# Rotary scores of the first attention in rounded high and low parts, with the query's high part copied across the partitions

## The reference, cut to what matters

```
q_nope, q_rope = q[..., :128], q[..., 128:]                       # per head, 128 and 64
q_rope, k_rope = axial_rope(q_rope, angles), axial_rope(k_rope, angles)
q = concatenate([q_nope, q_rope]);  k = concatenate([k_nope, broadcast(k_rope)])
s = einsum('bqhd,bkhd->bhqk', q, k) * (128 + 64) ** -0.5          # float32
p = softmax(s);  o = einsum('bhqk,bkhd->bqhd', p, v)
```

## Time and profile before

| | |
|---|---|
| median of three runs | 2628.06 us |
| profiled execution, its own time | 2628.91 us |
| its span (first to last instruction) | 2627.1 us |
| PE busy | 2589.2 us, 99% |
| DVE busy | 1780.0 us, 68% |
| ACT busy | 1212.4 us, 46% |
| mean data rate | 208 GB/s |
| mean granted clock of PE | 0.997 |

### The profile page before, as it was taken

One profiled execution on the slowest core, in us unless ns is written; L12 is line 12 of the kernel. 1 busy time (PEld: TensorE's weight loads), 2 busy tenths in 40 slices (PEclk: granted clock), 3 DMA queues, 4 the chain that ended last, 5 costly groups with the idle time before them and its releaser, 6 DMA issues.

```text
span 2627.1 us, 37181 instructions
## 1 busy us (share of the span) xinstructions
PE 2589.2 (99%) x15242; PEld 2236.1 (85%) x15242; DVE 1780.0 (68%) x2466; ACT 1212.4 (46%) x1595; POOL 33.4 (1%) x31
## 2 busy tenths in 40 slices
PE   6999999999999999999999999999999999999999
PEld 4788778888888888888888888899888888888888
DVE  4367977788888877555656676576766666665555
ACT  4442345455555555444433554445544444444443
POOL 2100000000000000000000000000000000000000
PEclk9999999999999999999999999999999999999999
DMA  9877864767777655556555543455555555555553
GB/s 391 345 300 268 327 236 163 234 212 240 235 239 235 211 192 185 190 194 192 186 185 191 165 134 136 160 184 193 185 192 189 189 192 186 192 191 190 188 191 121
DMA packets 151401, 547.21 MB, mean 208 GB/s; under 512 B 16960, under 2 KB 18880, under 8 KB 150464
## 3 DMA queue, kind: packets, MB, share of 16 engines
q1 hardware_dynamic: 148752, 540.35, 61.2%
q10 hardware_dynamic: 2480, 4.49, 0.6%
HBM read 542.68 MB, written 2.10 MB: 207 GB/s over the span
## 4 chain that ended last, share of the span: by engine, by line
PE 97%; DMA 2%; DVE 1%; issue 0%; ACT 0%; SPq 0%; ACTq 0%; DVEq 0%
PE ps L464 47%; PE ps L463 24%; PE ps L468 3%; PE ps L470 3%; PE ps L469 3%; PE ps L461 3%; PE ps L476 2%; PE ps L474 2%; PE ps L475 2%; DMA raw<-in_stream 2%; PE ps L462 1%; PE ps L1690 1%; PE ps L1899 1%; PE ps L1869 1%; PE ps L1871 1%; PE ps L1886 0%
## 5 line engine op out<-in xcount | busy, mean ns | idle before, releaser
L416 DVE TENSOR_TENSOR lo<-raw,hi 128x1024 fp32r<-128x1024 f32 x814 | 991.6, 1223 | 716.3 <-ACT hi L403 714.1
L464 PE MATMUL ps<-pair,hi 128*128 128x512 f32 x3994 | 1391.6, 392 | 0.0
L403 ACT ACTIVATE hi<-raw 128x1024 fp32r<-128x1024 f32 x814 | 859.5, 1059 | 1079.9 <-PE ps L464 908.3
L463 PE MATMUL ps<-pair,lo 128*128 128x256 f32 x3994 | 1120.0, 280 | 0.0
L464 PEld LDWEIGHTS ps<-pair,hi 128*128 128x128 f32 x3994 | 750.4, 188 | 161.4
L463 PEld LDWEIGHTS ps<-pair,lo 128*128 128x128 f32 x3994 | 750.6, 188 | 6.0 <-issue 2.4
L464 PE MATMUL ps<-hid,hi 128*128 128x512 f32 x1376 | 477.4, 392 | 0.0
L463 PE MATMUL ps<-hid,lo 128*128 128x256 f32 x1376 | 384.6, 280 | 0.0
L464 PEld LDWEIGHTS ps<-hid,hi 128*128 128x128 f32 x1376 | 258.3, 188 | 56.7
L463 PEld LDWEIGHTS ps<-hid,lo 128*128 128x128 f32 x1376 | 258.3, 188 | 0.3
L1288 DVE TENSOR_REDUCE tmp<-ps 128x256 f32<-128x512 f32 x260 | 176.6, 684 | 5.0 <-PE ps L464 4.6
(11 more groups left out here) (324 smaller groups left out, 2303.5 us busy)
## 6 DMA issues: line engine op xcount, KB each, us to landing
raw<-in_stream SPq DMA_DIRECT2D x983, 512.0 KB, 4.1
raw_deep<-in_stream SPq DMA_DIRECT2D x31, 512.0 KB, 10.9
xc<-in_xc SPq DMA_DIRECT2D x4, 1024.0 KB, 8.8
x<-in_x ACTq DMA_DIRECT2D x1, 2048.0 KB, 7.6
out<-out_sb SPq DMA_DIRECT2D x8, 256.0 KB, 2.9
c_bc<-in_c_bc SPq DMA_DIRECT2D x1, 1024.0 KB, 10.7
bias<-in_rpb ACTq DMA_DIRECT2D x4, 256.0 KB, 4.5
dft<-in_dft_tab ACTq DMA_DIRECT2D x1, 512.0 KB, 5.9
```

Source lines behind the costliest of these rows:

```text
L403: e.activation(hi[:, c % R, :], raw_of(p), ACT.Copy).then_inc(hi_ready, 1)
L416: e.tensor_tensor(lo[:, c % R, :], raw_of(p), hi[:, c % R, :].bitcast(F32), ALU.subtract)\
L463: e.matmul(out[:, T:2 * T], wlo, act[:, 0, :], start=False, stop=False)
L464: return e.matmul(out, whi, both_, start=False, stop=last)
```

## The change

The rotary part of a score is no longer one float32 matmul but two F32R ones. The key's rotary part is kept as its rounded high part `khigh` and as a stack `kstack`, with the high part on partitions 0 to 63 and the low part on 64 to 127. The query's high part is written for even heads into the lower half of `qeven` and for odd heads into the upper half of `qodd`, and a transfer copies it into the other half, so that one matmul of 128 rows gives high query by high key plus high query by low key. A matmul of 64 rows adds the query's low part by the key's high part.

- ACT: one copy less at `kr`; two copies that round the key behind the third square root of the statistics; behind `upto(at, "ukv", 2)` two copies of 64x1024 (`qeven`, `qodd`), a wait for them, and two transfers of 256 KB.
- DVE: one addition less for the key, one subtraction of 64x512 more (`kstack`'s low part); two subtractions of 64x1024 (`qrope_lo`) between `upto(at, "ukv", 4)` and the loop.
- PE: score 0 waits for `q_roped` 4 (was 2) and for the transfers; L1871 becomes two matmuls.
- GpSimd: the two memsets of `kre` and `kro` are gone.
- `q_sin` and `q_cos` become one semaphore, and `tok_sum` is replaced by a further count of `sq_sum`.

The buffers lie where earlier data is done with: `qeven` over `cqn`, `qodd` over `csil` and what follows it, `qrope_lo` over `qrope` itself.

```diff
@@ -267,8 +267,11 @@
         c_bc, _ = place("c_bc", [P, D], at=reg + 80 * K1)
         qnope, _ = place("qnope", [P, MLA_H, T], at=home)
         qrope, _ = place("qrope", [P, MLA_H // 2, T], at=home + 8 * K1)
-        kre, _ = place("kre", [P, 2, T], at=home + 12 * K1)
-        kro, _ = place("kro", [P, 2, T], at=home + 14 * K1)
+        qrope_lo, _ = place("qrope_lo", [P, MLA_H // 2, T], F32R, home + 8 * K1)
+        qeven, _ = place("qeven", [P, MLA_H // 2, T], F32R, reg + 48 * K1)
+        qodd, _ = place("qodd", [P, MLA_H // 2, T], F32R, csil_at)
+        kstack, _ = place("kstack", [P, 2, T], F32R, home + 12 * K1)
+        khigh, _ = place("khigh", [P, 2, T], F32R, home + 14 * K1)
 
         dft, _ = place("dft", [P, 4 * T], at=tmp_at)
         dft_c, _ = place("dft_c", [P, 2 * P], at=std_at)
...
@@ -343,9 +346,10 @@
                                                        sem("ckv_hi"), sem("ckv_lo"))
         c_stat, c_std, c_rinv = sem("c_stat"), sem("c_std"), sem("c_rinv")
         kr_copied, kr_turned, kr_mul, kr_roped = sem("kr_copied"), sem("kr_turned"), sem("kr_mul"), sem("kr_roped")
+        rope_hi, qr_moved = sem("rope_hi"), sem("qr_moved")
         kn_copied, vn_copied = sem("kn_copied"), sem("vn_copied")
         uq_copied, uk_copied, v_copied = sem("uq_copied"), sem("uk_copied"), sem("v_copied")
-        q_turned, q_sin, q_cos, q_roped = sem("q_turned"), sem("q_sin"), sem("q_cos"), sem("q_roped")
+        q_turned, q_mul, q_roped = sem("q_turned"), sem("q_mul"), sem("q_roped")
         qn_copied, f_copied = sem("qn_copied"), sem("f_copied")
         scores, biased, maxed, negmax = sem("scores"), sem("biased"), sem("maxed"), sem("negmax")
         exps, recips, probs = sem("exps"), sem("recips"), sem("probs")
...
@@ -649,10 +653,6 @@
         @block.gpsimd
         def _(e):
             e.memset(csil[:], 0.0).then_inc(zeroed, 1)
-            e.wait_ge(zeroed, 1)
-            e.memset(kre[64:P, :, :], 0.0).then_inc(zeroed, 1)
-            e.memset(kro[0:64, :, :], 0.0).then_inc(zeroed, 1)
-            e.wait_ge(zeroed, 3)
 
             for j, kt in enumerate(POOL_SQ):
                 e.wait_ge(sqx_piece, kt + 1)
...
@@ -752,11 +752,9 @@
                 return b
 
             e.wait_ge(weights_used, AT[("kr", 1)] + 1)
-            e.wait_ge(zeroed, 3)
             e.wait_ge(xc_lo, KT)
             e.activation(tmp[:, 0, :], half(6, 0), ACT.Copy).then_inc(kr_copied, 1)
-            e.activation(kre[0:64, 1, :], ps[0:64, 6, T:2 * T], ACT.Copy).then_inc(kr_copied, 1)
-            e.activation(kro[64:P, 1, :], ps[64:P, 6, T:2 * T], ACT.Copy).then_inc(kr_copied, 1)
+            e.activation(tmp[:, 3, :], half(6, 1), ACT.Copy).then_inc(kr_copied, 1)
             e.wait_ge(s_cbc_rope, 32)
             e.activation(c_bc[:], c_bc[:], ACT.Silu).then_inc(c_ready, 1)
             e.preload_act_table_set("sqrt_and_others")
...
@@ -773,6 +771,9 @@
             e.wait_ge(c_stat, 3)
             e.activation(small[:, 160:164], ps[:, 1, 0:4], ACT.Sqrt, bias=vec("eps"), scale=1.0 / RANK)\
                 .then_inc(c_std, 1)
+            e.wait_ge(kr_roped, 1)
+            e.activation(khigh[:], tmp[:, 2:4, :], ACT.Copy).then_inc(rope_hi, 1)
+            e.activation(kstack[0:ROPE], tmp[0:ROPE, 2:4, :], ACT.Copy).then_inc(rope_hi, 1)
             at = upto(at, "vn", CPG - 1)
             e.wait_ge(weights_used, BASE["vn"] + CPG)
             for tt in range(4):
...
@@ -783,6 +784,12 @@
                 e.dma_start(bias[(r % 2) * GRID_W:(r % 2 + 1) * GRID_W, :, r // 2, :], src).then_inc(s_bias, 16)
             e.dma_start(mask[:], na_mask).then_inc(s_bias, 16)
             at = upto(at, "ukv", 2)
+            e.wait_ge(q_roped, 2)
+            e.activation(qeven[0:ROPE], qrope[0:ROPE], ACT.Copy).then_inc(rope_hi, 1)
+            e.activation(qodd[ROPE:P], qrope[ROPE:P], ACT.Copy).then_inc(rope_hi, 1)
+            e.wait_ge(rope_hi, 4)
+            e.dma_start(qeven[ROPE:P].bitcast(F32), qeven[0:ROPE].bitcast(F32)).then_inc(qr_moved, 16)
+            e.dma_start(qodd[0:ROPE].bitcast(F32), qodd[ROPE:P].bitcast(F32)).then_inc(qr_moved, 16)
             for gg in range(2):
                 e.wait_ge(weights_used, BASE["ukv"] + 2 * (gg + 1))
                 e.wait_ge(c_rinv, 3)
...
@@ -1172,19 +1179,20 @@
 
             at = upto(at, "vn", 5)
             e.wait_ge(s_cbc_rope, 32)
-            e.wait_ge(kr_copied, 3)
+            e.wait_ge(kr_copied, 2)
             e.tensor_tensor(tmp[:, 1, :], tmp[:, 0, :], cos, ALU.mult).then_inc(kr_mul, 1)
             e.wait_ge(kr_turned, 1)
             e.tensor_tensor(tmp[:, 2, :], half(2, 0), sin, ALU.mult).then_inc(kr_mul, 1)
             e.wait_ge(kr_mul, 2)
-            e.tensor_tensor(kre[0:64, 0, :], tmp[0:64, 1, :], tmp[0:64, 2, :], ALU.add).then_inc(kr_roped, 1)
-            e.tensor_tensor(kro[64:P, 0, :], tmp[64:P, 1, :], tmp[64:P, 2, :], ALU.add).then_inc(kr_roped, 1)
+            e.tensor_tensor(tmp[:, 2, :], tmp[:, 1, :], tmp[:, 2, :], ALU.add).then_inc(kr_roped, 1)
             e.wait_ge(c_std, 3)
             e.reciprocal(std[:], std[:]).then_inc(c_rinv, 1)
             at = upto(at, "vn", 6)
             e.reciprocal(rinv[:], rinv[:]).then_inc(c_rinv, 1)
             at = upto(at, "vn", 7)
             e.reciprocal(small[:, 160:164], small[:, 160:164]).then_inc(c_rinv, 1)
+            e.wait_ge(rope_hi, 2)
+            e.tensor_tensor(kstack[ROPE:P], tmp[ROPE:P, 2:4, :], khigh[ROPE:P].bitcast(F32), ALU.subtract).then_inc(kr_roped, 1)
             at = upto(at, "vn", CPG)
             e.wait_ge(c_rinv, 3)
             for g in range(6):
...
@@ -1210,13 +1218,15 @@
                         e.wait_ge(q_turned, 2 * b + 2)
                         q = qrope[:, 2 * b:2 * b + 2, :]
                         e.tensor_tensor(tmp[:, 2 * b:2 * b + 2, :], by_two(ps[:, 3 + b, :]),
-                                        sin.unsqueeze(1).to_broadcast([P, 2, T]), ALU.mult).then_inc(q_sin, 1)
-                        e.tensor_tensor(q, q, cos.unsqueeze(1).to_broadcast([P, 2, T]), ALU.mult).then_inc(q_cos, 1)
-                        e.wait_ge(q_sin, b + 1)
-                        e.wait_ge(q_cos, b + 1)
+                                        sin.unsqueeze(1).to_broadcast([P, 2, T]), ALU.mult).then_inc(q_mul, 1)
+                        e.tensor_tensor(q, q, cos.unsqueeze(1).to_broadcast([P, 2, T]), ALU.mult).then_inc(q_mul, 1)
+                        e.wait_ge(q_mul, 2 * b + 2)
                         e.tensor_tensor(q, q, tmp[:, 2 * b:2 * b + 2, :], ALU.add).then_inc(q_roped, 1)
                 at = upto(at, "ukn", g + 1)
             at = upto(at, "ukv", 4)
+            e.wait_ge(rope_hi, 4)
+            e.tensor_tensor(qrope_lo[0:ROPE], qrope[0:ROPE], qeven[0:ROPE].bitcast(F32), ALU.subtract).then_inc(q_roped, 1)
+            e.tensor_tensor(qrope_lo[ROPE:P], qrope[ROPE:P], qodd[ROPE:P].bitcast(F32), ALU.subtract).then_inc(q_roped, 1)
 
             N = 2 * HEADS
             def om_low(c):
...
@@ -1863,12 +1873,14 @@
                     e.wait_ge(biased, 2 * (n - 3 - 2 * MLA_H + 1))
                 if h < MLA_H:
                     if n == 0:
-                        e.wait_ge(q_roped, 2)
+                        e.wait_ge(q_roped, 4)
                         e.wait_ge(uk_copied, MLA_H)
                         e.wait_ge(kr_roped, 2)
+                        e.wait_ge(qr_moved, 32)
                     e.matmul(by_two(out), qnope[:, h, q], knope(h), start=True, stop=False)
-                    kr = kro if h % 2 else kre
-                    m = e.matmul(out, qrope[:, h // 2, q], kr[:].rearrange("p s t -> p (s t)"), start=False, stop=True)
+                    r = slice(ROPE * (h % 2), ROPE * (h % 2 + 1))
+                    e.matmul(by_two(out), (qodd if h % 2 else qeven)[:, h // 2, q], kstack[:], start=False, stop=False)
+                    m = e.matmul(by_two(out), qrope_lo[r, h // 2, q], khigh[r], start=False, stop=True)
                 else:
                     if n == 2 * MLA_H:
                         e.wait_ge(qn_copied, 2)
```

## The result

The changed kernel takes 2638.27 us (median of 6 runs, 2637.49 to 2639.73), the one before 2628.07 us (2628.05 to 2628.19): ratio 1.0039, 95% interval 1.0029 to 1.0049, 10.2 us slower. Forecast were 3.2 us. The profiled execution is the fastest of the six, 2637.49 us with a span of 2635.7; that of before was itself 0.85 us above its median, so between the two profiles only 8.6 us are to be found.

What follows compares the result with a forecast made beforehand. TensorE (PE) was taken as the bound, with 97% of the chain. -6.2 (matmuls) + 7.05 (wait before score 0) + 2.4 (half clock) = +3.2 us on 2628.06, so 2631.3 us; own range 2630.0 to 2633.0, wider range 2628.6 to 2634.2.

Steps and rivals of the forecast that it cites:

- the first term of the sum: First attention's 16 scores on PE: two F32R matmuls replace one float32, saving 0.389 us per score, -6.2 us.
- The stop: PE before score 0 waits for DVE's two query subtractions, queued behind chunk f3's work: +7.05 us (5.5 to 7.1).
- The clock: PE behind the wait before score 0: half clock for about five microseconds of dense work, +2.4 us (nothing to 3.4).
- The other edits: nothing: ACT's query and key copies, the transfers, DVE's key work, GpSimd memsets and a renamed semaphore: no cost.
- the steps with masks: Attention steps where DVE also masks the bias: DVE close to the bound, nothing counted; 1 us if it bounds.
- (a): Before score 0, PE waits but its clock doesn't fall: +0.8 us, 2628.9 us; chance 10%.
- (b): Before score 0, DVE's subtractions don't hold PE back, only the saving is left: 2621.9 us, faster; chance 5%.
- (c): Before score 0, the transfer ends last, not DVE, and PE stops 12.6 us: +8.8 us, 2636.9 us; chance 7%.
- (d): As forecast, but DVE bounds the mask steps (1 us) and the clock takes 3.4: +5.3 us, 2633.3; chance 8%.
- The bound "nothing" for the saving: Scores on PE: lower bound of the saving, if two F32R matmuls are as dear as one float32; upper bound 10.0 us.

Runs made afterwards that it cites:

- x4: Changed kernel with 30 useless F32R matmuls filling PE's wait for the query's low part before score 0: 2635.70 us, ratio 1.0030 to the kernel before.
- x1: Changed kernel with the third matmul of each score over all 128 rows instead of 64 (scores not the reference's): 2633.13 us, ratio 1.0018 to the kernel before.
- x3: Changed kernel with the stacked 128-row matmul replaced by two of 64 rows, so three 64-row matmuls per score: 2644.39 us, ratio 1.0061 to the kernel before.
- x2: Changed kernel with DVE's two query low-part subtractions moved ahead of the work on chunks f2 and f3: 2631.32 us, ratio 1.0010 to the kernel before.
- x5: x2 without the two transfers and PE's wait for them, ACT's copies writing all 128 partitions instead: 2627.87 us, ratio 0.9998 to the kernel before.
- x8: x1 and x5 together, third matmul over 128 rows and no transfers: 2622.43 us, ratio 0.9979 to the kernel before.
- b1: Changed kernel with x2's order, third matmul of 128 rows against a zero-padded high key, query copies and transfers one chunk earlier: 2623.82 us, ratio 0.9984.

## Why the prediction was wrong

The step that failed is the first term of the sum, -6.2 us for the rotary matmuls. It measured 0: scores without a mix come 4.96 us apart where it was 4.95, and at full clock (x4) the whole way from the first score to the neighbourhood heads is 104.2 us where it was 104.1. It failed in the sentence "That one of them has only 64 rows should not matter". That sentence rested on the second of a run of 64-row matmuls, at 1487.57 us in the earlier trace rows. The lines on both sides of it, in the same chain of the kernel before, tell the opposite:

```profile
1487.15 0.41 PE ps L2145 x2
...
1488.00 0.22 PE ps L2145 x2
1488.22 0.43 PE ps L2146 x2
1488.66 0.31 PE ps L463
```

The first 64-row matmul takes 0.41 us and its twin 0.22; the first 128-row one behind takes 0.31 where L463 takes 0.12 elsewhere. That is 0.19 us in and 0.19 out, the price that x1 and x3 show (0.43 for 0.23). Twice 0.2 us is the 0.39 us that each score was to save.

The other steps, in order. The stop: 7.2 us for 7.05, its cause and every piece of it right. The clock: +2.4 us in the profile, 2.6 by x4, for +2.4. "The other edits: nothing": right for ACT's and DVE's work, wrong for the transfers. They landed 7.0 and 8.8 us after issue, before DVE was done, as said; but behind DVE's stop they would have been the next to be late (x2, 1.7 us), and in some executions the weights of f3 come late (x1 and x3), which x5, without the transfers, does not show. The medians were 10.2 us apart where stop and clock give 9.6 to 9.8; the rest of 0.4 to 0.6 fits stops of 8.2 and 8.8 us as profiled in x3 and x1, but the slower executions of the changed kernel itself were not profiled. DVE kept up in the steps with masks. Rivals (a) and (b) did not happen; (c) did not decide, but x2 has its mechanism; (d) foresaw no loss of the gain. With 0 in the place of -6.2 the sum is +9.45 us, 2637.5, which is the profiled execution. That this meets it so closely is luck: the profiled execution is the fastest of six, 0.8 us below the median, and its PE reached score 0 about 1 us sooner than that of before. The bound "nothing" for the saving was named in the text, and the range did not reach to it.

The rule of the Trainium skill on four passes ("FP8 and Floating Point Precision") would have given a saving of 7.5 us; with full rows the runs show 6.0 (x1) and 5.6 (x8), so 0.856 us for the float32 matmul was the better figure. The one that bears on the failed step is in "TensorE: Matmul & The Clock Gate" (Part 3, What overlaps and what doesn't, and step 1 of Part 2): weight loads are pulled ahead of a running matmul when their rows of the array don't conflict or a spare weight buffer takes them. The traces agree in part: 128-row loads are pulled ahead of 128-row matmuls, and 64-row ones of each other (x3), but not across a change from one to the other. The same page holds that the number of rows does not matter for the time of a load; the traces agree, 0.18 us for 64 rows and 0.19 for 128.

## What to carry to other kernels

Price a short matmul by the lines at the edges of a group of its kind, where it meets others, and not by one from the middle; and where all neighbours have 128 rows, fill it up with zeros to 128. What PE waits for must stand, in its engine's order, ahead of work that itself waits for PE; one call's difference cost 9.6 us here, of which x2 won back 7.0. A transfer between partitions beside a full weight stream cost more here than its bytes, and the first sign was scatter between runs.

## What the runs showed of the hardware that was not expected

The two transfers of 256 KB move 0.52 MB. In b1, from 289.5 to 302 us, the shares of the DMA engines are these (packets, MB, share):

```profile
q1 hardware_dynamic: 769, 2.81, 79.7%
q10 hardware_dynamic: 160, 0.52, 17.6%
```

and before, from 285 to 302 us:

```profile
q1 hardware_dynamic: 1658, 6.03, 95.5%
```

Together 3.33 MB in 12.5 us are 266 GB/s, where the stream alone ran at 6.03 MB in 17 us, 355 GB/s. At that rate 12.5 us would have brought 4.4 MB; 1.6 MB of weights were put back, three times what the transfers moved. Without the transfers, in x5, the stream moves this from 289.5 to 302 us:

```profile
q1 hardware_dynamic: 1266, 4.63, 96.6%
```

In the changed kernel the loss is smaller: from 294.3 to 303.7 us its stream moved 2.56 MB, where 3.67 were moved before, 1.1 MB less or twice the 0.52. The stream's own packets took longer as well: by share, length and count, one held an engine for 0.16 us before and for 0.21 in b1. Why was not tried.
